# Four column orders for the moving operand of the main matmuls, and weights at four places

## The reference

```python
h = rmsnorm(x, g[0])
proj = h @ w_in[l]                                   # 2048 x 6736
...
up = jnp.einsum('bsnc,ncd->bsnd', branches, w_branch[l])
gates = jax.nn.sigmoid((h @ w_gate[l]).reshape(B, S, N_BRANCHES, D) + b_gate[l])
mixed = jnp.sum(gates * up, axis=2) @ w_out[l]
x = x + rmsnorm(mixed, g[1])
h = rmsnorm(x, g[2])
m = jnp.square(jax.nn.relu(h @ w_up[l])) @ w_down[l]  # 2048 x 8192, 8192 x 2048
x = x + rmsnorm(m, g[3])
...                                                   # second block:
p = h @ w_l                                           # 2048 x 9216
attn = _attention(q, jnp.concatenate([k, kc], axis=1), jnp.concatenate([v, vc], axis=1))
y_a = (attn * jax.nn.silu(z_a)) @ w_pa
y_b = (_fourier_mix(u_b) * jax.nn.silu(z_b)) @ w_pb
y = (g_a * y_a + g_b * y_b) @ w_o
```

## Time and profile before

| | before |
|---|---|
| median of 2 runs | 2342.5 us (2341.75 to 2343.25) |
| the profiled execution: time, span | 2343.5 us, 2341.7 us |
| mean granted TensorE clock | 0.997 |
| TensorE matmul busy | 2312.0 us, 99% |
| VectorE, ScalarE busy | 1469.0 us, 63%; 1070.9 us, 46% |
| DMA | 473.73 MB, 202 GB/s |

### The profile page before, as it was taken

The page is one execution under the profiler, slowest core; times in us unless marked ns, Lnnn a source line. Parts: engine busy times, 40 slices in busy tenths (PEclk is TensorE's granted clock), DMA queues, the critical chain, the costliest instruction groups (busy, mean ns, idle before and its releaser), DMA issues.

```text
span 2341.7 us, 37604 instructions
## 1 busy us (share of the span) xinstructions
PE 2312.0 (99%) x15980; PEld 2152.9 (92%) x15980; DVE 1469.0 (63%) x1844; ACT 1070.9 (46%) x1422; POOL 40.4 (2%) x61
## 2 busy tenths in 40 slices
PE   7999999999999999999999999999999999999998
PEld 7989999999999988988988988998899979999986
DVE  6757477777787667544555555555755545676665
ACT  5344435444344456444443443444655545433443
POOL 1000000000000001000000000000100000000000
PEclk9999999999999999999999999999999999999999
DMA  8855676677777765656656556556764444778763
GB/s 268 248 162 157 187 215 218 217 224 233 245 226 254 251 222 172 180 196 190 180 193 194 181 188 204 183 191 195 237 179 144 145 126 127 258 255 266 237 203 139
DMA packets 246368, 473.73 MB, mean 202 GB/s; under 512 B 21166, under 2 KB 25624, under 8 KB 244536
## 3 DMA queue, kind: packets, MB, share of 16 engines
q1 hardware_dynamic: 242888, 454.40, 61.1%
q0 software_dynamic: 3312, 16.92, 2.2%
HBM read 467.05 MB, written 4.21 MB: 201 GB/s over the span
## 4 chain that ended last, share of the span: by engine, by line
PE 97%; DVE 1%; issue 1%; ACT 0%; DMA 0%; SPq 0%; POOL 0%; POOLq 0%; DVEq 0%; ACTq 0%
PE ps L860 20%; PE ps L861 20%; PE ps L862 20%; PE ps L853 10%; PE ps L855 10%; PE ps L854 10%; PE ps L788 1%; PE ps L727 1%; PE ps L623 1%; PE ps L649 1%; PE ps L767 0%; PE ps L768 0%; PE ps L777 0%; PE ps L801 0%; PE ps L664 0%
## 5 line engine op out<-in xcount | busy, mean ns | idle before, releaser
L1220 DVE TENSOR_TENSOR wlo<-raw,whi 128x1024 fp32r<-128x1024 f32 (+1 forms) x768 | 927.5, 1216 | 736.9 <-ACT whi L892 735.7
L892 ACT ACTIVATE whi<-raw 128x1024 fp32r<-128x1024 f32 (+1 forms) x768 | 802.9, 1053 | 962.5 <-PE ps L862 618.2
L860 PE MATMUL ps<-op0h,whi 128*128 128x256 f32 x3248 | 927.7, 286 | 1.1 <-DVE wlo L1220 1.1
L861 PE MATMUL ps<-op0l,whi 128*128 128x256 f32 x3248 | 919.7, 283 | 0.0
L862 PE MATMUL ps<-op0h,wlo 128*128 128x256 f32 x3248 | 919.6, 283 | 0.0
L860 PEld LDWEIGHTS ps<-op0h,whi 128*128 128x128 f32 x3248 | 623.9, 192 | 6.4 <-issue 5.8
L861 PEld LDWEIGHTS ps<-op0l,whi 128*128 128x128 f32 x3248 | 624.1, 192 | 2.0 <-issue 1.4
L862 PEld LDWEIGHTS ps<-op0h,wlo 128*128 128x128 f32 x3248 | 623.9, 192 | 0.0
L853 PE MATMUL ps<-whi,op1h 128*128 128x512 f32 x640 | 249.5, 390 | 0.0
L854 PE MATMUL ps<-wlo,op1h 128*128 128x512 f32 x640 | 249.0, 389 | 0.0
L855 PE MATMUL ps<-whi,op1l 128*128 128x512 f32 x640 | 249.0, 389 | 0.0
(11 more groups left out here) (262 smaller groups left out, 1911.2 us busy)
## 6 DMA issues: line engine op xcount, KB each, us to landing
raw<-in_w_in SPq DMA_DIRECT2D x256, 512.0 KB, 4.2
raw<-in_w_up SPq DMA_DIRECT2D x128, 512.0 KB, 3.7
raw<-in_w_down SPq DMA_DIRECT2D x128, 512.0 KB, 4.0
raw<-in_w_ada SPq DMA_DIRECT2D x96, 512.0 KB, 4.6
raw<-in_w_gate SPq DMA_DIRECT2D x96, 512.0 KB, 4.6
raw<-in_w_out SPq DMA_DIRECT2D x64, 512.0 KB, 4.4
raw<-in_w_branch SPq DMA_DIRECT2D x48, 512.0 KB, 5.0
raw<-in_w_proj_a SPq DMA_DIRECT2D x24, 512.0 KB, 4.2
```

Source lines behind the costliest of these rows:

```text
L860: pe.matmul(o, wh, xh[:, ka, :], start=first and m % 2 == 0, stop=False, skip_group_check=True)
L861: pe.matmul(o, wh, xl[:, ka, :], start=False, stop=False, skip_group_check=True)
L892: act.activation(whi[q % NSPL][:, :, 0:job.n], raw[i][:, :, 0:job.n], ACT.Copy).then_inc(s_hi, 1)
L1220: v.tensor_tensor(wlo[q % NSPL][:, :, 0:job.n], x, h.bitcast(F32), ALU.subtract).then_inc(s_lo, 1)
```

## The change

It does three things. First, each chunk whose job has 512 columns reads its moving operand, and writes PSUM, in one of four orders, by `(q + q // 16) % 4`: 0, straight; 1, pieces of 16 columns (64 bytes) from the first and the second half of the row in turn; 2, pieces of 16 columns that stand 256 bytes apart, first all the first ones, then all the second ones, and so on; 3, like 1 with 32 columns (128 bytes). Moving operand and output are permuted alike, so each column's result lands where it did. Second, the weight buffers are made 192 bytes longer, and the chunk stands at 0, 64, 128 or 192 bytes into the buffer, by `q // 4 % 4`. Third, `op0` now starts at remainder 0 modulo 256, `op1` at 64 and `big` at 128; `a5` becomes another name for `tmp[5]`.

```diff
-        whi = [sb(f"whi{i}", [128, KC, 512], F32R) for i in range(NSPL)]
-        wlo = [sb(f"wlo{i}", [128, KC, 512], F32R) for i in range(NSPL)]
-        op0_at = top[0]
+        def line(shift):
+
+            top[0] += (shift - top[0]) % 256
+            return top[0]
+
+        def split_buffers(name):
+
+            w = []
+            for i in range(NSPL):
+                o = line(0)
+                w.append([at(f"{name}{i}{s}", [128, KC, 512], o + 64 * s, F32R) for s in range(4)])
+                top[0] = o + 192 + 4 * KC * 512
+            return w
+
+        whi, wlo = split_buffers("whi"), split_buffers("wlo")
+        op0_at = line(0)
...
-        op1_at = top[0]
+        op1_at = line(64)
...
-        a5 = sb("a5", [128, 512])
+        a5 = tmp[5]
...
-        big = top[0]
+        big = line(128)
...
-                h, l = whi[q % NSPL], wlo[q % NSPL]
+                order = (q + q // 16) % 4 if job.n == 512 else 0
+
+                def m_(x):
+
+                    if order == 1:
+                        return x.rearrange("p (h l e) -> p l h e", h=2, e=16)
+                    if order == 2:
+                        return x.rearrange("p (x b e) -> p b x e", b=4, e=16)
+                    if order == 3:
+                        return x.rearrange("p (h l e) -> p l h e", h=2, e=32)
+                    return x
+
+                h, l = whi[q % NSPL][q // 4 % 4], wlo[q % NSPL][q // 4 % 4]
...
-                            pe.matmul(o, th, h[:, kk, 0:job.n], start=first, stop=False, skip_group_check=True)
+                            pe.matmul(o, th, m_(h[:, kk, 0:job.n]), start=first, stop=False, skip_group_check=True)
...
-                            pe.matmul(o, wh, xh[:, ka, :], start=first and m % 2 == 0, stop=False, skip_group_check=True)
+                            pe.matmul(o, wh, m_(xh[:, ka, :]), start=first and m % 2 == 0, stop=False, skip_group_check=True)
...
-                act.activation(whi[q % NSPL][:, :, 0:job.n], raw[i][:, :, 0:job.n], ACT.Copy).then_inc(s_hi, 1)
+                act.activation(whi[q % NSPL][q // 4 % 4][:, :, 0:job.n], raw[i][:, :, 0:job.n], ACT.Copy).then_inc(s_hi, 1)
```

More of the change, by code:

```diff
@@ L850, in chunk @@
                         for tt in tts:
-                            o = banks[tt][:, 0:job.n]
+                            o = m_(banks[tt][:, 0:job.n])
                             th, tl = xh[:, ka, 128 * tt:128 * tt + 128], xl[:, ka, 128 * tt:128 * tt + 128]
-                            pe.matmul(o, th, h[:, kk, 0:job.n], start=first, stop=False, skip_group_check=True)
-                            pe.matmul(o, th, l[:, kk, 0:job.n], start=False, stop=False, skip_group_check=True)
-                            mm = pe.matmul(o, tl, h[:, kk, 0:job.n], start=False, stop=last, skip_group_check=True)
+                            pe.matmul(o, th, m_(h[:, kk, 0:job.n]), start=first, stop=False, skip_group_check=True)
+                            pe.matmul(o, th, m_(l[:, kk, 0:job.n]), start=False, stop=False, skip_group_check=True)
+                            mm = pe.matmul(o, tl, m_(h[:, kk, 0:job.n]), start=False, stop=last, skip_group_check=True)
                     else:
                         for m in range(job.n // 128):
-                            o = banks[m // 2][:, 256 * (m % 2):256 * (m % 2) + 256]
+                            o = m_(banks[m // 2][:, 256 * (m % 2):256 * (m % 2) + 256])
                             wh, wl = h[:, kk, 128 * m:128 * m + 128], l[:, kk, 128 * m:128 * m + 128]
-                            pe.matmul(o, wh, xh[:, ka, :], start=first and m % 2 == 0, stop=False, skip_group_check=True)
-                            pe.matmul(o, wh, xl[:, ka, :], start=False, stop=False, skip_group_check=True)
-                            mm = pe.matmul(o, wl, xh[:, ka, :], start=False, stop=last, skip_group_check=True)
+                            pe.matmul(o, wh, m_(xh[:, ka, :]), start=first and m % 2 == 0, stop=False, skip_group_check=True)
+                            pe.matmul(o, wh, m_(xl[:, ka, :]), start=False, stop=False, skip_group_check=True)
+                            mm = pe.matmul(o, wl, m_(xh[:, ka, :]), start=False, stop=last, skip_group_check=True)
                 if 1 in tts:
@@ L1217, in low @@
                 job = chunks[q][0]
-                x, h = raw[landed["w", q][0]][:, :, 0:job.n], whi[q % NSPL][:, :, 0:job.n]
+                x, h = raw[landed["w", q][0]][:, :, 0:job.n], whi[q % NSPL][q // 4 % 4][:, :, 0:job.n]
                 v.wait_ge(s_hi, q + 1)
-                v.tensor_tensor(wlo[q % NSPL][:, :, 0:job.n], x, h.bitcast(F32), ALU.subtract).then_inc(s_lo, 1)
+                v.tensor_tensor(wlo[q % NSPL][q // 4 % 4][:, :, 0:job.n], x, h.bitcast(F32), ALU.subtract).then_inc(s_lo, 1)
             summed = [0, 0]
```

## The result

The changed kernel takes 2364.5 us (2 runs, 2364.24 to 2364.77) beside 2342.5 before: ratio 1.0094, interval 1.007 to 1.0119. The forecast was 2322. The change is as small as forecast, but its sign is the other one; and the interval holds no 1, so a change under 2%, which the prediction took for not measurable, can be told here.

A forecast was written before the change was run, and what follows sets the result against it. TensorE bounds the kernel: number of matmuls times the step between starts. Terms of -15.8, +2.0, -4.0 and -2.2 us sum to -20 us, giving 2322 us against the median 2342.5; range 2250 to 2470.

The forecast's parts named there:

- I take zero on top of the straight order: All 512-column jobs: the three reordered reads cost the same as the straight one, 0 ns extra per matmul.
- a meeting of the two reads of SBUF: TensorE matmuls: moving columns and next weights' load collide by place modulo 256, costing 6.7 to 15.7 ns over the columns.
- Places in mode W: 256-column matmuls: four weight places average to 118.6 ns; op0 and op1 -15.8 us, yah +2.0 us.
- Places in mode T: 512-column matmuls: four weight places average to 225.2 ns; op0 and op1 -4.0 us, mgh and hch -2.2 us.
- at 0 the two modes agree: Excess at moving minus stationary 0 is 13.3 ns in mode W, 13.4 in T, so T's 15.7 at 64 was carried over.
- Nothing else moved: All engines: same instructions and waits, sharing a5 with tmp[5] costs nothing, moved buffers give VectorE and ScalarE the same sizes.
- Halves free of the load: Orders of halves lose the excess at three places of four: -84 us, 2258 us; chance 0.27.
- Each piece costs: Piece ends in moving read or PSUM write: 182 us per ns, 2398 us and up; 0.31, including lingering with a price.
- 256 bytes apart linger: Order with pieces 256 bytes apart meets the load twice as dearly: +50 us, 2372; alone, within the 0.42.
- Places don't matter: yah's 6.7 ns has another cause, so the time stays 2342 us; chance 0.08, within the 0.42.

The follow-up runs named there:

- places alone: Changed kernel with all chunks read straight; weights at four places and moved operand buffers stay: 2329.93 us, ratio 0.9951 to the kernel before.
- a place for each mode: Changed kernel, but all straight, moving minus stationary 192 bytes in mode W and 0 in mode T: 2301.55 us, ratio 0.9827 to the kernel before.
- halves, moving operand alone: Changed kernel with buffer remainders of before; every 512-column job reads its moving operand in order 1, output written straight: 2388.11 us, beside 2345.82 before.
- output alone: Changed kernel with buffer remainders of before; every 512-column job writes PSUM in order 1, moving operand read straight: 2345.58 us, beside 2345.82 before.
- short loads: Kernel of orders alone, second and third matmul of each product using only 32 stationary columns and writing 32 partitions: 2357.01 us.
- orders alone: Changed kernel with its four orders, but moving operands and weights at the remainders modulo 256 of before: 2362.19 us, ratio 1.0085 to the kernel before.

## Why the prediction was wrong

- **The step that failed** is the one on the four orders: "I take zero on top of the straight order". It was argued from a meeting with the load: each order reads every piece once, a quarter at each remainder. Measured, the orders bring mode T with op1 from 228 to 233 ns straight up to 236 to 240, at every place; after against places alone, that is +17.9 us (27.6 - 9.7). In mode W they hold the step at 118 to 120 at every place, which takes back 15.8 of the 22.5 us that the places give. Together +33.7 us where zero stood; without it the sign would have been right.
- **The cause behind it**, "a meeting of the two reads of SBUF", was half right. That the place of the moving operand against the weights counts is shown (places alone, a place for each mode, where mgh's 228.9 ns fell to 226.7 as well). But the price of the orders is shown to be in the moving read (halves, moving operand alone: 240.0; output alone: 226.7), and it keeps its size beside short loads. Why a pair of places costs what it does isn't shown.
- **Places in mode W** were right in sign, and their near size is in part luck. For 0, 64, 128 and 192 the prediction's excesses give 120.0, 122.4, 118.6 and 113.3 ns; places alone gave 119.9, 117.7, 118.8 and 115.3 with op0. The excess carried over from mode T to 64 was 4.7 ns too high, and yah's 113.3, one of the two values that 192 has, 2.0 too low; together the mean is 117.9 in place of 118.6. The term was -13.8 and measured -22.5: 0.7 ns of 11,280 matmuls are 7.9 of the 8.7 us between the two.
- **Places in mode T** had the wrong sign, -6.2 forecast, +9.7 measured. Two excesses were carried from one mode to the other, since "at 0 the two modes agree". At 192 mode W has 6.7 or 11.0 ns, its cheapest place, and mode T 20.0 (233.3), its dearest. As shares of the columns the modes don't agree at 0 either: 13.3 of 106.7 is an eighth, 13.4 of 213.3 a sixteenth. Order 1 makes it an eighth in both, 120.0 and 240.0. That fits mode W losing nothing by it at 0 and mode T 13.3 ns, but why a straight read pays twice the share in mode W isn't shown.
- **Nothing else moved** was right: sharing a5, the waits, clock and other engines cost nothing.
- **The rivals.** *Halves free of the load* is refuted: order 1 is the dearest order, not the cheapest. *Each piece costs* gave the right sign by the wrong mechanism: 7 boundaries of 256-byte pieces cost nothing. By the Trainium skill (SBUF - State Buffer, Door 1: The DMA port swizzle) a non-contiguous PSUM pattern significantly slows matmuls; with 64-byte pieces the output alone gave 2345.58 us beside 2345.82, so no run here shows it for pieces of this size. *256 bytes apart linger* is refuted: in mode T that order is dearer than straight, but orders 1 and 3 are as dear, and in mode W at 0 it is cheaper (118.3 ns, orders alone). *Places don't matter* is refuted by a place for each mode, ratio 0.9827. The Trainium skill (TensorE: Matmul & The Clock Gate, Step-by-step: what each phase is for) has two independent read ports; that a shorter load doesn't speed up a matmul in order 1 (240.0 ns) agrees with it, that the straight step hangs on the weights' remainder (120.0 or 113.3 ns) doesn't.

## What to carry to other kernels

Where TensorE sets the time, measure the step from start to start for each kind of matmul and each remainder modulo 256 of its two operands, and don't carry an excess from one shape to another: here the best place of one mode is the worst of the other, and the right one for each was worth 1.7%. Read the moving operand straight, or in pieces of 256 bytes, which cost nothing here. Shorter pieces at place 0 took 230.8 to 243.3 ns in mode T for 226.7, and 117.9 to 123.3 in mode W for 120.0; an output in 64-byte pieces cost nothing. A step that the trace doesn't show gets no "zero" from an argument of symmetry: a zero needs a row.

## What the runs showed that was not expected

- At one place (192) a straight matmul of 256 columns has two steady steps, 113.3 and 117.7 ns, for whole stretches, with the same instructions and operands. What chooses between them is open; were all 323 chunks of 117.7 in the kernel with a place for each mode at 113.3, 323 x 24 x 4.4 ns, an estimate of 34 us, would go.
- Loads of 0.11 us in place of 0.19 make mode W faster (116.7 for 120.0 ns) and mode T slower (230.0 for 226.7).
- Order 1 takes 120.0 and 240.0 ns, 1.125 times the columns; pieces of 8 columns go above that (123.3 and 243.3).
